# Inverting 64x64 triangular blocks on Trainium2: block placement that uses four quarters of TensorE's array, and copies over contiguous columns

## The reference, cut to what matters

```python
def gated_delta_chunked(q, k, v, g, beta):        # chunks of c = 64 tokens
    ...
    d_incl = jnp.exp(jnp.where(incl, diff, -jnp.inf))
    d_strict = jnp.where(strict, d_incl, 0.0)
    a_mat = beta[..., :, None] * jnp.einsum('nhcid,nhcjd->nhcij', k, k) * d_strict
    gam = jnp.exp(cum)
    rhs = jnp.concatenate([beta[..., None] * v, (beta * gam)[..., None] * k], axis=-1)
    sol = lax.linalg.triangular_solve(a_mat, rhs, left_side=True, lower=True, unit_diagonal=True)
    u0, w = sol[..., :dv], sol[..., dv:]
    p_intra = jnp.einsum('nhcid,nhcjd->nhcij', q, k) * d_incl
    ...
```

## Time and profile before

| what | value |
|---|---|
| runs | 1997.73, 1992.64, 1995.97 us; median 1995.97 |
| profiled execution, span from first to last instruction | 2001.2 us (no other time is given for it) |
| TensorE busy, share of the span | 1764.2 us, 88% |
| VectorE, ScalarE, GpSimd busy | 857.6, 592.7, 243.5 us |
| mean granted clock of TensorE | 0.964 of 2.4 GHz |
| inverse's products (line 525), first and last start | 935.5 and 1748.0 us |
| their TensorE busy time | 215.5 us |

### The profile page before, as it was taken

One profiled execution on the slowest core, in us unless ns is written; L12 is line 12 of the kernel. 1 busy time (PEld: TensorE's weight loads), 2 busy tenths in 40 slices (PEclk: granted clock), 3 DMA queues, 4 the chain that ended last, 5 costly groups with the idle time before them and its releaser, 6 DMA issues.

```text
span 2001.2 us, 44027 instructions
## 1 busy us (share of the span) xinstructions
PE 1764.2 (88%) x17970; PEld 1033.3 (52%) x17970; DVE 857.6 (43%) x1514; ACT 592.7 (30%) x1018; POOL 243.5 (12%) x270
## 2 busy tenths in 40 slices
PE   5998895977778877898999899999989998899996
PEld 2444543544444444445865784354447856853452
DVE  1567524111111111367666753151457747642331
ACT  3314521000000000334324424252253325424442
POOL 0002211111111111006112100001002103000001
PEclk8998996999999999998999999999999999999998
DMA  9758025999999999521000003110211000012101
GB/s 358 259 197 291 1 69 220 370 423 424 423 424 424 425 424 413 216 74 33 3 3 2 3 20 109 42 43 32 80 43 35 3 2 2 4 65 104 42 1 42
DMA packets 75098, 307.75 MB, mean 154 GB/s; under 512 B 10908, under 2 KB 22300, under 8 KB 57888
## 3 DMA queue, kind: packets, MB, share of 16 engines
q1 hardware_dynamic: 63280, 291.98, 37.2%
q0 software_dynamic: 5360, 9.33, 1.3%
q10 hardware_dynamic: 6272, 3.81, 0.6%
HBM read 301.01 MB, written 16.52 MB: 159 GB/s over the span
## 4 chain that ended last, share of the span: by engine, by line
PE 73%; DVE 13%; another core or an unknown queue 6%; ACT 4%; issue 3%; DMA 1%; DVEq 0%; ACTq 0%; POOL 0%; POOLq 0%
PE bank L2253 12%; PE bank L496 12%; PE bank L2269 6%; PE bank L1027 6%; PE bank L525 5%; PE bank L532 4%; PE bank L2091 3%; PE bank L2175 3%; PE bank L998 2%; DVE arena L1596 2%; ACT arena L1039 1%; PE bank L512 1%; PE bank L2115 1%; PE bank L2103 1%
## 5 line engine op out<-in xcount | busy, mean ns | idle before, releaser
L496 PE MATMUL bank<-hT,arena 128*128 128x512 f32 (+1 forms) x640 | 287.7, 605 | 3.6 <-ACTq L1040 2.4
L2253 PE MATMUL bank<-arena 128*64 128x256 f32 x1792 | 216.3, 399 | 66.9 <-remote 66.9
L525 PE MATMUL bank<-arena 64*64 64x64 f32 x6656 | 215.5, 220 | 22.7 <-DVE arena L1726 7.2
L525 PEld LDWEIGHTS bank<-arena 64*64 64x64 f32 x6656 | 203.8, 136 | 37.0 <-DVE arena L1726 10.1
L2253 PEld LDWEIGHTS bank<-arena 128*64 128x64 f32 x1792 | 135.6, 143 | 158.0 <-issue 107.8
L496 PEld LDWEIGHTS bank<-hT,arena 128*128 128x128 f32 (+1 forms) x640 | 122.9, 194 | 161.2 <-issue 156.6
L2859 DVE COPY arena<-bank 128x256 f32<-128x256 f32 x32 | 13.6, 425 | 329.6 <-PE bank L2261 329.6
L2269 PE MATMUL bank<-arena 128*64 128x512 f32 x448 | 104.0, 606 | 16.4 <-remote 16.4
L1027 PE MATMUL bank<-arena 128*128 128x512 f32 x256 | 110.4, 593 | 0.0
L1039 ACT ACTIVATE arena<-bank 128x512 f32<-128x512 f32 (+2 forms) x124 | 73.2, 590 | 118.9 <-PE bank L496 79.2
L532 PE MATMUL bank<-hT,arena 128*128 128x512 f32 x224 | 105.0, 607 | 1.7 <-remote 1.7
(11 more groups left out here) (448 smaller groups left out, 2677.1 us busy)
## 6 DMA issues: line engine op xcount, KB each, us to landing
arena<-w_gate SPq DMA_DIRECT2D x28, 2048.0 KB, 30.6
arena<-w_up SPq DMA_DIRECT2D x28, 2048.0 KB, 21.0
arena<-w_down SPq DMA_DIRECT2D x28, 2048.0 KB, 26.2
arena<-w_ada SPq DMA_DIRECT2D x12, 2048.0 KB, 19.7
arena<-w_in SPq DMA_DIRECT2D x10, 2048.0 KB, 11.7
arena<-w_out SPq DMA_DIRECT2D x6, 2048.0 KB, 7.6
arena<-w_in SPq DMA_DIRECT2D x6, 1536.0 KB, 6.9
hT<-w_up SPq DMA_DIRECT2D x4, 2048.0 KB, 20.9
```

Source lines behind the costliest of these rows:

```text
L496: m = pe.matmul(bank[b][0:w, :], slot2(n)[:, k, c:c + w], hT[:, k, :], start=(k == 0), stop=(k == KD - 1))
L525: m = pe.matmul(o[half(f), s, t], lhs[half(f), s, t], rhs[half(f), s, t], start=True, stop=True)
L2253: mm = pe.matmul(bank[b][c * CAP:(c + 1) * CAP, 0:FE // 2], XT[j][:, k % 4, k // 4, :], e_slot(e_at(e, i), KD)[:, k, c * (FE // 2):(c + 1) ...
```

## The change

The 16 small matrices of a tile get other places, and the products other quarters.

- **Places.** `placed()` reads the 512 columns as (g, s, h, 64), `g` being the partition half in which a block's *partner* of a product lies; chunk (t, f) has g = (t mod 2) xor f and h = t div 2 (`block_of`). Half of the blocks have g = f, half g = 1 - f.
- **Across.** V is computed from input half `f` into output half `g`, into bank `2d + f`, columns 0 to 255: all four (f, g) pairs occur, in the order (0,0), (1,1), (0,1), (1,0).
- **Back.** The product with Y goes from half `g` home to half `f`, into bank `2d + g`, the same 256 columns. For blocks whose V lies in the other half Y is needed there too: ScalarE copies these 64x256 pieces of Y, one from each half, to the other half, into `y_far` (in the tile `rs`), before each level, `changed_half`. TensorE waits for them (`y_far_full`).
- **Banks.** V and the result back of a direction now share two banks (0 and 1, 2 and 3) instead of having one each. The products u0 go to banks 0 and 2, the decay rows of later blocks to 1 and 3, the third tile of values to 0. TensorE waits in level 1 of GDN ahead of the product across for all banks of the direction, where it waited ahead of the product back for one.
- **Columns.** Copies and elementwise operations that ran over pieces of 64 columns run over 128 or 256 in a row (`by_head`, `two`). The sign of B in GDN moves into the copy of V. Four tiny copies per layer lay out the keys' decays (`g_k2`).
- RWKV's u0 keeps the old two quarters, in a loop of its own.

```diff
+        g_k2 = g_ln.rearrange("p t c -> p (t c)")[:, 0:48].rearrange("p (k g s h) -> p k g s h", k=6, g=2, s=2)
+        y_far = [rs[:, 256 * d:256 * d + 256] for d in range(2)]
...
+        def placed(ap):
+            return ap.rearrange("p (g s h n) -> p g s h n", g=2, s=2, h=2)
+        def block_of(ap, f, s, t):
+            return placed(ap)[half(f), (t % 2) ^ f, s, t // 2]
+        def by_head(ap):
+            return ap.rearrange("p (g s m) -> p s g m", g=2, s=2)
+        def of_banks(b, k):
+            return banks[:, b:b + 2, 256 * k:256 * k + 256].rearrange("p s (g m) -> p s g m", g=2)
+        def two(ap):
+            return ap.rearrange("p (g m) -> p g m", g=2)
...
-            def product(b, lhs, rhs):
-
-                o, lhs, rhs = pieces(bank[b]), pieces(lhs), pieces(rhs)
+            quarters_of = ((0, 0), (1, 1), (0, 1), (1, 0))
+            def across(d, lhs, rhs):
+
+                lhs, rhs = placed(lhs), placed(rhs)
                 for s in range(2):
-                    for t, f in pairs_in:
-                        m = pe.matmul(o[half(f), s, t], lhs[half(f), s, t], rhs[half(f), s, t], start=True, stop=True)
+                    for h in range(2):
+                        for f, g in quarters_of:
+                            o = bank[2 * d + f][half(g), (2 * s + h) * CG:(2 * s + h + 1) * CG]
+                            m = pe.matmul(o, lhs[half(f), g, s, h], rhs[half(f), g, s, h], start=True, stop=True)
+                return m
+            def back(d, Y, V, last):
+
+                Y, V = placed(Y), placed(V)
+                for s in range(2):
+                    for h in range(2):
+                        cols = slice((2 * s + h) * CG, (2 * s + h + 1) * CG)
+                        for g, f in quarters_of:
+                            y = Y[half(g), g, s, h] if f == g else y_far[d][half(g), cols]
+                            v = V[half(g), f, s, h]
+                            m = pe.matmul(bank[2 * d + g][half(f), cols], v if last else y, y if last else v, start=True, stop=True)
                 return m
...
                     for l in range(1, LEVELS):
                         for d in range(2):
                             t_full[d].wait()
-                            product(d, g_Bn[d], g_T[d]).then_inc(sem(f"g_v_done{d}"), 1)
+                            if l == 1:
+                                for b in (2 * d, 2 * d + 1):
+                                    pe.wait_ge(bank_free[b], 1)
+                            across(d, g_Bn[d], g_T[d]).then_inc(sem(f"g_v_done{d}"), 1)
                         for d in range(2):
+                            far_full[d].wait(2)
                             v_full[d].wait()
-                            y_full[d].wait()
-                            if l == 1:
-                                pe.wait_ge(bank_free[2 + d], 1)
-                            if l < LEVELS - 1:
-                                product(2 + d, g_Y[d], g_V[d]).then_inc(sem(f"g_t_done{d}"), 1)
-                            else:
-                                product(2 + d, g_V[d], g_Y[d]).then_inc(sem(f"g_t_done{d}"), 1)
+                            back(d, g_Y[d], g_V[d], l == LEVELS - 1).then_inc(sem(f"g_t_done{d}"), 1)
...
+            def product_moved(d, V, sign):
+
+                act.activation(two(V), banks[:, 2 * d:2 * d + 2, 0:256], ACT.Copy, scale=sign).then_inc(sem(f"g_v_full{d}"), 1)
+            def changed_half(d, Y):
+
+                for g in range(2):
+                    act.activation(y_far[d][half(g)], Y[half(1 - g), 256 * g:256 * g + 256], ACT.Copy)\
+                       .then_inc(sem(f"y_far_full{d}"), 1)
...
                     if ht == 1:
-                        values(2, 3)
-                        raw(6, 2)
-                    if ht == 2:
-                        raw(2, 2)
+                        values(2, 0)
+                    for d in range(2):
+                        y_full[d].wait()
+                        changed_half(d, g_Y[d])
+                    if ht > 0:
+                        raw((6, 2)[ht - 1], 2)
                     for l in range(1, LEVELS):
                         for d in range(2):
+                            if l > 1:
+                                y_full[d].wait()
+                                changed_half(d, g_Y[d])
                             v_done[d].wait()
                             if l == 1:
                                 pt_full[d].wait()
-                            act.activation(g_V[d], bank[d], ACT.Copy).then_inc(sem(f"g_v_full{d}"), 1)
+                            product_moved(d, g_V[d], -1.0)
...
                         for f in range(2):
+                            for g in range(2):
+                                chain.mark(dve.tensor_copy(g_k2[half(f), :, g], g_c2[half(f), g ^ f:TT:2].rearrange("p h (k s) -> p k s h", s=2)))
...
+                def take_over(d, dst, l, upper):
+
+                    return dve.copy_predicated(two(dst), merged(d, l, upper), banks[:, 2 * d:2 * d + 2, 0:256])
```

126 lines of the change are left out of this document (68 added, 58 removed).

## The result

The changed kernel takes **2011.02 us** (2008.55 to 2016.63, 4 runs) where the kernel before takes 1996.22 (4 runs): a ratio of 1.0081, 95% interval 1.0064 to 1.0098. It is slower by 0.8%; 1977 was forecast. The profiled execution spans 2014.8 us, 13.6 more than before.

What follows compares the result with a forecast made beforehand. TensorE's load (4.07 us) and the level's loop of waits (4.36) were taken to bound nearly equally. 17.0 from plain levels plus 3.6 at block starts less 1.4 for copies gave 19.2 us less: 1977, range 1965 to 1990.

Steps and rivals of the forecast that it cites:

- The rate of the products: Levels of the inverse on TensorE: records 0.0141 us apart instead of 0.0303, a new product priced at 0.47 us plus 0.22.
- the quarters don't help: Rival, 7%: new products in the levels still run at 0.0303 us per record; about 1999, no change.
- The loop of a plain level: Round of waits through TensorE, VectorE and ScalarE in a plain level: falls from 4.33 to 3.62 us, by 0.71.
- the price of the half copies: ScalarE's added copies of Y per direction and level: 0.41 us each, 0.74 the pair, bounds 0.6 and 1.25.
- 24 intervals: Level-to-level intervals, both layers, that can shrink: 0.71 us each, 17.0 us in all; the other 16 give nothing.
- Starts and ends of blocks: First two products of a block gain about 0.6 us in six blocks, 3.6 us; nothing in GDN's second and third blocks.
- u and w: GDN's products behind a block's levels (lines 641 and 649): no change forecast.
- The work in front of blocks: Eight tiny copies into g_k2 in a block's preparation, where VectorE is waited for: 1.4 us added.
- The rule weighed: Copies out of PSUM may bind after a TensorE speed-up; pace by busiest engine's load gives 2.8 us levels, 1958; not adopted.
- TensorE's clock falls: Rival, 6%: levels run at clock 0.50, 8 us more, work between blocks begins slow, 10 us more; about 2014.
- The half copies are dear: Rival, 12%: half copies in the levels cost 0.62 us each, loop 4.13 us; 7 us less in all, 1989.

Runs made afterwards that it cites:

- e3: Changed kernel without half copies of Y or the waits for them, still four quarters (result not the inverse, timing only); 1994.85 us, ratio 0.9986 to the kernel before.
- e10: Four quarters with half copies on GpSimd in blocks 1, 2, 6 and 7, two quarters without half copies elsewhere; 1995.42 us, ratio 0.9993 to the kernel before.
- e8: Changed kernel with the half copies of blocks 1, 2, 6 and 7 on GpSimd; 2011.20 us, ratio 1.0085 to the kernel before.
- e15: Changed kernel with direction 0's copy of V ahead of direction 1's half copies in level 1, GDN's first block and RWKV; 2013.79 us.
- e14: Changed kernel with eight unread 64x64 matmuls once per layer ahead of GDN's first block, shifting the instruction list; 2016.04 us, ratio 1.0108 to the kernel before.
- e9: Changed kernel with the 1.5 MB weight load held back until the last level of GDN's first block; 2012.85 us, ratio 1.0095 to the kernel before.
- e1: Changed kernel with unread 128x128 by 256-column filler matmuls behind the levels' products; 2037.08 us, ratio 1.0209 to the kernel before.
- e11: Changed kernel on two quarters without half copies, plus two semaphore clears ahead of each of a product's 16 matmuls; 2642.85 us.

## Why the prediction was wrong, point by point

The sum was 19.2 us less; the profiled execution shows 13.6 more, 32.8 apart.

- **The rate of the products** was right: 0.48 us from first to last record for 0.47. The rival "the quarters don't help" falls.
- **The loop of a plain level**, forecast 3.62, is 3.88. Along the rows above: up to the take-over 0.75 (0.72 forecast), take-over 0.77 (0.77), transpose and hand-over 0.75 (0.75), the pair of half copies 0.87 (0.74), copy of V with hand-over 0.74 (0.64). Two terms were mis-sized: the two half copies do not overlap (0.85, twice 0.415; the length of one was right to 0.005), and TensorE starts 0.14 behind the copy of V, not 0.04. On the 20 plainest intervals that makes 8.5 us of gain out of 14.2.
- **The steps that failed** are two. The first is the price of the half copies: 3.62 in place of 3.36 in 24 intervals, 6.2 us, and nothing at the starts and ends of blocks. The changed kernel less e3 shows 21.3 us: 8.5 on the 20 plainest intervals, 1.4 on the other 20, 11.4 at the starts and ends. The second is that TensorE's work is ready to run whenever its data is, so that a faster loop stays a faster loop. Without half copies the prediction's own terms (24 x 0.97 + 3.6) give 26.9 us of gain in the levels; e3 has 16.3. In the changed kernel the 20 plainest intervals gave 5.4 us, and the other 20, priced at -2.8, gave +3.0. Blocks 2, 4, 7 and 9 have intervals of 4.5 to 5.3 with a stall each, block 0 5.90 and block 5 5.55. The list itself had to come, and I did not look at q8 in the profile of before at all. So of the 32.8 us apart 15.1 are the half copies', 10.6 the levels' without them, 9.1 lie in u and w, and -2.0 between blocks and after.
- **Starts and ends of blocks**, forecast at -3.6, gave +7.5. In e3 they gave -4.0, so the forecast held without the half copies. In level 1 both pairs of them stand in ScalarE's order ahead of both copies of V; ScalarE at the start of block 0:

```profile
936.37 1.73 ACT L1132 ACTIVATE rs<-arena 64x256 f32<-64x256 f32 x4
938.13 1.08 ACT L1128 ACTIVATE arena<-bank 128x512 f32<-128x512 f32 x2
```

  From the first product across to the first product back it is 4.33 us there, before 2.90, in e3 2.63. In blocks 1, 2, 6 and 7 the order costs nothing (2.35 us, in e3 too), since there the copies of V come behind the eviction in any case.
- **u and w**, forecast at nothing, gave +9.1. Timelines of u (line 641) behind block 1 in the changed kernel, then in e10 (line 646), with w (line 654) behind it:

```profile
997.10 3.37 PE L641 MATMUL bank<-arena 64*64 64x64 f32 x62
```

```profile
992.32 2.12 PE L646 MATMUL bank<-arena 64*64 64x64 f32 x61
...
994.33 0.64 PE L654 MATMUL bank<-arena,sq 64*64 64x64 f32 x30
995.53 0.69 PE L654 MATMUL bank<-arena,sq 64*64 64x64 f32 x32 [0.56 <-issue]
```

  u is +5.7 in sum: 5.0 in blocks 0, 1, 2 and 5, where it ran at 0.50 wholly or in part (3.0 to 3.2 us in place of 1.85), and 0.6 in block 8, where the clock was 1.00 and it has a stall. w is +2.5, stalls as in the second fence, and 0.9 lie between its last record and the next product (w alone is at 0.0147 per record, the rate of the new products, and follows them without a wait).
- **The work in front of blocks**, +1.4, does not show: between blocks it is -0.2.
- **The rule weighed** (the Trainium skill, TensorEngine Tiling (Array Packing), PSUM Bottleneck) was rightly not taken for a load: no engine is full in the new level. But copies that TensorE waits for did become the largest idle time ahead of line 555, 38.4 us, as that page warns.
- **The rival "TensorE's clock falls"** had 6% and gave 2014, near the 2011 measured. Its condition did not hold: in plain levels without a stall the clock is 1.00, as I had argued against it. What it describes came only in part: 61 us at 0.50, in ten stretches. Three of them, 13.6 us, begin behind a stall (one at 1170.8, straight behind that of 1170.45). The other seven do not: block 3 has 17.1 us at 0.50 and no stall at all, in blocks 0 and 5 the clock fell ahead of the first stall, and three lie over u. That it hits the work between blocks, 10 us by that rival, came true with 5.0. It has nearly the right number by luck: of the 32.8 us only these 5.0 are shown to be the clock's. By the Trainium skill (TensorE: Matmul & The Clock Gate, HAM oscillation) it is idle gaps of TensorE that bring the clock down; the trace agrees in kind (TensorE busy for 1.83 of the 3.40 us ahead of the fall at 1126.4), with gaps that are mostly waits for ScalarE and VectorE and in part stops of the instruction list.
- **"The half copies are dear"** had 1.25 us a pair and 1989; the pair is 0.85, and in the plain loop it costs 0.46. They are dear all the same, 21 us in the levels, but by other ways than this rival's: over half of it at the starts and ends of blocks.

Shown are: half copies in the loop and at the starts (e3, e8, e15), stalls from the list (e14), the collision with a load (e9), and that u and w lose with four quarters only (the table). Open is how the 10.6 us in the levels split between the stalls and the clock: e1 took both away at once, and nothing here took away one alone. Open too are what starts a fetch and the 5 us that all versions share. Four quarters within one bank per direction was not tried.

## What to carry to other kernels

Before making small matmuls faster, count instructions as well as columns: look for the packets of the instruction queue in the profile, how many instructions each holds, how long from a fetch's start to its first instruction, and whether the faster stretch uses up a packet in less time. A helper copy is cheap only where it isn't in the loop; the same half copies cost 0.46 us a level on ScalarE, ahead of the copy of V, and nothing on an idle engine beside it. Work that a change doesn't touch, behind the part that it makes faster, can lose what that part won: measure it as a term of its own.

## What was not expected of the hardware

- TensorE stops at boundaries of 256 instructions in its list when it gets there less than 2.2 to 3.0 us after a fetch of the next 16 KB began; the stops here are 0.1 to 1.5 us, and 1.3 to 4.4 beside or just behind a weight load at 400 GB/s.
- `sem_clear` between matmuls of TensorE costs 0.10 us each, also where the semaphore is zero already; two of them and a matmul of 64x64x64 take 0.25 us at either clock (e11).
- A matmul with a 64x1 stationary among those with 64x64 makes the pair cost 0.37 us in place of 0.06 at clock 1.00, and 0.52 in place of 0.11 at 0.50.
- A matmul of 128x128 by 256 float32 columns took 0.69 us here, at clock 1.00 (e1).
- Two copies of 64x256 on ScalarE follow each other at 0.43 us with no overlap; on GpSimd the pair takes the same 0.85.
